# The first block's output projection in high and low parts instead of full-width fp32 products

## What is computed

```python
mod = silu(c) @ w_ada + b_ada            # six vectors of 1024: sh1, sc1, g1, sh2, sc2, g2
merged = concatenate([rmsnorm(lru_out), rmsnorm(attn_out)], axis=-1)    # 256 x 1024
y = merged @ w_out                        # 1024 x 1024, fp32
x = layernorm(DEEPNORM_ALPHA * x + g1 * y)
u = modulate(x, sh2, sc2)                 # input of the mixture of experts
```

## Time and profile before

| | before |
|---|---|
| device time, median of 3 runs | 3467.67 us |
| lowest and highest of them | 3466.52 and 3473.76 us |
| the profiled execution: first to last instruction | 3464.7 us |
| TensorE busy, VectorE busy, ScalarE busy | 91%, 67%, 46% |
| this stage, first DMA issue to the last residual instruction | 191.3 to 226.7 us |

### The profile page before, as it was taken

How to read it: one execution, slowest core, us unless ns; L and a number is a source line. 1 busy time by engine, 2 the same in 40 slices (tenths; PEclk the granted TensorE clock), 3 DMA queues, 4 the chain that set the end, 5 groups by cost and what they waited for, 6 DMA issues and landing times. The chain is left out here.

```text
span 3464.7 us, 62893 instructions
## 1 busy us (share of the span) xinstructions
PE 3157.3 (91%) x26416; PEld 2942.4 (85%) x26416; DVE 2335.4 (67%) x3486; ACT 1580.8 (46%) x2255; POOL 130.5 (4%) x148
## 2 busy tenths in 40 slices
PE   7679999889987799999989899999899999978899
PEld 5568777789876789999987899999699998867899
DVE  6547999767774467677577577775667677564544
ACT  3326777644551244544552444444644444432443
POOL 0000000000102000000000000000000001011000
PEclk9778999989997989999996899999899999989899
DMA  9336999757520047677430277675157575310242
GB/s 391 138 134 263 368 370 365 291 211 303 204 104 2 2 191 305 244 289 295 173 146 1 116 281 277 249 303 194 40 226 303 224 304 227 112 38 2 110 183 85
DMA packets 74502, 698.32 MB, mean 202 GB/s; under 512 B 8096, under 2 KB 12192, under 8 KB 50848
## 3 DMA queue, kind: packets, MB, share of 16 engines
q1 hardware_dynamic: 31360, 533.52, 39.3%
q10 hardware_dynamic: 41760, 153.11, 11.6%
q0 software_dynamic: 1152, 8.39, 0.6%
HBM read 690.79 MB, written 4.19 MB: 201 GB/s over the span
## 5 line engine op out<-in xcount | busy, mean ns | idle before, releaser
L1186 DVE TENSOR_TENSOR w_split<-ring,w_split 128x1024 fp32r<-128x1024 f32 x513 | 626.3, 1223 | 407.6 <-ACT w_split L1097 405.1
L1097 ACT ACTIVATE w_split<-ring 128x1024 fp32r<-128x1024 f32 x513 | 540.6, 1056 | 774.7 <-PE banks L1027 580.6
L1025 PE MATMUL banks<-u_split,w_split 128*128 128x256 f32 x2816 | 805.7, 286 | 14.7 <-DVE u_split L1246 12.9
L1026 PE MATMUL banks<-u_split,w_split 128*128 128x256 f32 x2816 | 803.8, 285 | 0.0
L1027 PE MATMUL banks<-u_split,w_split 128*128 128x256 f32 x2816 | 803.5, 285 | 0.0
L1025 PEld LDWEIGHTS banks<-u_split,w_split 128*128 128x128 f32 x2816 | 548.2, 195 | 19.4 <-DVE w_split L1186 10.0
L1026 PEld LDWEIGHTS banks<-u_split,w_split 128*128 128x128 f32 x2816 | 548.1, 195 | 0.4
L1027 PEld LDWEIGHTS banks<-u_split,w_split 128*128 128x128 f32 x2816 | 547.7, 195 | 0.0
L584 DVE CUSTOM_DVE_ANT_0 bufs<-bufs 128x1024 f32<-128x1024 f32 x332 | 395.0, 1226 | 41.9 <-DMA bufs<-ada 25.0
L1025 PE MATMUL banks<-h_split,w_split 128*128 128x256 f32 x1408 | 398.7, 283 | 1.8 <-DVE w_split L1186 1.8
L1026 PE MATMUL banks<-h_split,w_split 128*128 128x256 f32 x1408 | 398.4, 283 | 0.0
(11 more groups left out here) (472 smaller groups left out, 5067.5 us busy)
## 6 DMA issues: line engine op xcount, KB each, us to landing
ring<-stream SPq DMA_DIRECT2D x155, 3072.0 KB, 10.9
bufs<-ada ACTq DMA_DIRECT2D x288, 512.0 KB, 10.6
bufs<-ada SPq DMA_DIRECT2D x7, 2048.0 KB, 11.9
bufs<-ada POOLq DMA_DIRECT2D x8, 1024.0 KB, 8.3
ring<-stream SPq DMA_DIRECT2D x2, 2688.0 KB, 9.7
bufs<-c_rows SPq DMA_DIRECT2D x9, 512.0 KB, 4.5
ring<-stream SPq DMA_DIRECT2D x1, 2704.0 KB, 12.9
ring<-stream SPq DMA_DIRECT2D x1, 2176.0 KB, 7.8
```

The lines of the kernel that those rows point to most:

```text
L1025: pe.matmul(out, w(0), x(0), start=start, stop=False, skip_group_check=True)
L1026: pe.matmul(out, w(0), x(1), start=False, stop=False, skip_group_check=True)
L1097: nc.scalar.activation(w_split[:, slot, 0, :], piece(j, b), ACT.Copy).then_inc(high.sem, 1)
L1186: e = nc.vector.tensor_tensor(w_split[:, slot, 1, :], piece(j, b), w_split[:, slot, 0, :].bitcast(F32), ALU.subtract)
```

## The change

The projection is done in high and low parts. TensorE makes 192 products in fp32r (24 a block) in place of 64 in fp32. ScalarE, which had nothing in this stage, makes four high parts of the activations (128x512 each) and eight of the weights. VectorE makes four low parts of the activations, in place over `merged`, and eight of the weights: those of blocks 0 to 2 ahead of the modulation sums, those of blocks 3 to 7 between the quarters: behind the second and fourth quarter of slabs one and two and behind the second of slab three. SP's list is as it was. What `project_first_pair`, `project_split`, `weight_high` and `weight_low` do is described above.

```diff
@@ first_output_stage @@
+    high, low, w_slots = core.split_buf(1), core.split_buf(0), core.weight_slots(2)
+    keys = [("w_out", j) for j in range(KC)]
...
         @block.tensor
         def _(pe):
-            for j in range(KC):
-                core.project(pe, ("w_out", j), lambda k: merged[:, k, :], y[:, j, :], projected)
+            project_first_pair(core, pe, keys[0:2], w_slots, (high, low), core.psum[:, 0, :], u_low, projected, per=2)
+            for b in range(2, KC):
+                project_split(core, pe, b, keys[b], w_slots, (high, low), y[:, b, :], projected)
             after.on_tensor(pe)
+
+        @block.scalar
+        def _(act):
+            for c in range(0, KC, 2):
+                act.activation(high[:, c:c + 2, :], merged[:, c:c + 2, :], ACT.Copy).then_inc(u_high.sem, u_high.count(1))
+                if c in (0, 2):
+                    weight_high(core, act, c // 2, keys[c // 2], w_slots, projected)
+            for b in range(2, KC):
+                weight_high(core, act, b, keys[b], w_slots, projected)
 
         @block.vector
         def _(dve):
             link = chain(core, dve, "dve")
             pre(dve, link)
+            for c in range(0, KC, 2):
+                dve.wait_ge(u_high.sem, u_high.at(c // 2 + 1))
+                dve.tensor_tensor(low[:, c:c + 2, :], merged[:, c:c + 2, :], high[:, c:c + 2, :].bitcast(F32), ALU.subtract)\
+                    .then_inc(u_low.sem, u_low.count(1))
+                if c in (0, 2):
+                    weight_low(core, dve, c // 2, keys[c // 2], w_slots)
+            weight_low(core, dve, 2, keys[2], w_slots)
             for k in range(count):
                 dve.wait_ge(ada_loaded[k % 2].sem, ada_loaded[k % 2].at(16 * (k // 2 + 1)))
                 for q in range(4):
                     at = 4 * (first + k) + q
                     ada_quarter(core, dve, q, slots[k % 2], c_row, core.mod_sums[:, at:at + 1])
+                    if q in (1, 3) and 2 * k + q // 2 < KC - 3:
+                        weight_low(core, dve, 2 * k + q // 2 + 3, keys[2 * k + q // 2 + 3], w_slots)
```

More of the change, by code:

```diff
@@ L1664, in first_output_stage @@
     first, count = FIRST_HALVES + SECOND_HALVES, 12 - FIRST_HALVES - SECOND_HALVES
+    high, low, w_slots = core.split_buf(1), core.split_buf(0), core.weight_slots(2)
+    keys = [("w_out", j) for j in range(KC)]
     with core.nc.Block() as block:
         projected, step = core.event("projected"), core.event("ada_step")
+        u_high, u_low = core.event("u_high"), core.event("u_low")
         ada_loaded = [core.event(f"ada_loaded{q}") for q in range(2)]
```

## The result

| | before | changed |
|---|---|---|
| device time, median of 12 runs | 3463.51 us | 3474.61 us |
| ratio of changed to before | | 1.0038 (1.0024 to 1.0051) |
| the same, compared a second time | | 1.0026 (1.0015 to 1.0037) |
| profiled execution, first to last instruction | 3464.7 us | 3471.8 us |

The change makes the kernel slower by 0.26 to 0.38%, 9 to 13 us. The prediction was 3476.4 us in a range of 3470.0 to 3479.5, 8.75 us over before. One run of the changed kernel took 8920.83 us, over twice the others; it is left out of the ratios. (The brackets behind a ratio are its 95% interval.)

What follows compares the result with a forecast made beforehand. The prediction took VectorE's chain through SP's slab requests to bound the projection stage. A residual 5.6 us later plus token sums 3.15 us slower made 8.75 us on a median of 3467.67: 3476.4 us, range 3470 to 3479.5.

Steps and rivals of the forecast that it cites:

- What bounds the stage: Projection stage: VectorE's chain through SP's requests for slabs three and four ends it, within 1 us of TensorE's chain.
- TensorE's part: Projection products: first one 4.87 us after the stage's start, last near 223.2; even with VectorE free only 0.9 us to win.
- The head of VectorE's list at no cost: Before slab one: seven low parts, 5.8 us, fit inside VectorE's wait of 7.28 us and cost nothing.
- The wait for the fourth high part: After two quarters of slab one: VectorE idles 3.1 us for ScalarE, delaying SP's requests for slabs three and four.
- Slab four's landing: End of VectorE's chain: slab four lands 8.56 us after its request, at 224.25, so the residual starts 5.6 us later.
- The clock: Token sums behind the projection: TensorE's clock falls in a 6.4 us pause, so they take 6.90 us, adding 3.15 us.
- the chance of 0.2 for its holding: Rival for the token sums: the clock stays full through the pause, saving 3.15 us, result 3473.3 us; chance 0.2.
- Sum: Whole kernel: 5.6 us for the later residual plus 3.15 us for slower token sums, 8.75 us, giving 3476.4 us.
- Rival 2: VectorE's low part of block 3: no stall for its high part, 2.7 us cost, 3470.4 or 3473.5 us; chance 0.12.
- rival 3: Whole kernel faster: TensorE's own end moves by 0.9 us, to 3466.8 us at best; chance 0.03.
- rival 4: Projection blocks at half clock: more stalls, TensorE ends the stage at 229 to 234.8, 3476 to 3482 us; chance 0.07.

Runs made afterwards that it cites:

- three_slabs_fp32: The kernel before (fp32 products) with a third buffer for the slabs of modulation weights; ratio 0.9988, 65.32 us for the stage and the norms behind it.
- no_late_low_parts: The changed kernel without the low parts of weight blocks 3 to 7 and TensorE's products of them; ratio 1.0025, 69.98 us for stage and norms.
- changed_again: The changed kernel itself, unaltered, compared with the kernel before a second time; ratio 1.0026, 75.38 us for stage and norms.
- clock_fillers: The changed kernel with 40 products of zeros on TensorE between its last product and the token sums; ratio 1.0002, 72.85 us for stage and norms.
- more_high_slots: The changed kernel with five slots for the weights' high parts instead of three; ratio 1.0023, 72.39 us for stage and norms.
- norm_fillers: three_slabs_fp32 with products of zeros in TensorE's pauses in the centre stages behind the projection; ratio 0.9973, 65.35 us for stage and norms.
- split_three_slabs: The changed kernel with a third slab buffer, a fourth high-part slot and low parts 3 to 7 moved; ratio 0.9997, 70.30 us for stage and norms.

## Why the prediction was right

**What bounds the stage.** Right: VectorE's chain through SP's requests. three_slabs_fp32 shows it by removing the wait for a buffer.

**TensorE's part.** Right. First product 4.9 us after the stage's start (worked out 4.87), last one ended at 223.4 (223.2).

**The head of VectorE's list at no cost.** Right, and no_late_low_parts shows it alone. The margin was 0.45 us, not the 1.4 worked out, because slab one landed in 7.65 us instead of 8.56.

**The wait for the fourth high part.** Right in place, cause and size: the low part starts at 205.27 (205.28), after 3.62 us (3.1, slab one being earlier). SP's requests fell at 208.81 and 215.66 (208.8 and 215.7). The stage started 0.28 us later in this execution, so counted from its start each of these came 0.3 us sooner than worked out.

**Slab four's landing.** This term was too large. I took 8.56 us, the load with another behind it; it took 7.80, near the lower of the bounds. The Trainium skill says that on each DMA engine the descriptors of one row's ring are consumed in order (DMA: Bandwidth & Descriptors, "Queues, rings and completion order"), and the trace agrees: with the 3 MB unit requested 0.37 us behind it slab four took 7.80 us, as slab three took 7.77 with nothing behind it. It took 7.84, 7.83 and 7.93 us in changed_again, clock_fillers and no_late_low_parts, but 8.56 in more_high_slots, which none of my runs explains. I had let slab one's row speak against the rule. It isn't chance alone: slab one reached VectorE 7.64 to 7.80 us after its request in six executions of split kernels, slab two just as close behind, but after 8.56 us in the kernel before. With a third slab requested behind them it was 9.12 and 9.52 us with fp32 products (three_slabs_fp32, norm_fillers), and at most 8.26 in the two split kernels. So a row of the fp32 form was a poor price for the split form; why the two differ stays open. With the stage's later start of 0.28 us the term is 4.52 us for 5.6.

**The clock.** Right in size, 3.26 us for 3.15, and clock_fillers shows the cause. That it fell in the pause was in part luck. I had worked out a pause of 6.4 us, and it was 5.40, inside the 5.2 to 5.9 us where by my own figures either could happen. The 5.9 was misread, too: it is the length of TensorE's pause there, and the mean of 0.85 from 3226 to 3229 puts the fall at 3228.1, 5.3 us after the last work at 3222.75. So no pause of the trace had held the clock for 5.9 us, and the chance of 0.2 for its holding leaned on that. It fell 4.7 us after the last product here (223.4 to 228.1), and 3.5 and 2.7 us after it in more_high_slots and split_three_slabs. So a pause of 2.05 us cost 2.7 us in the sums (6.46 against 3.73), nearly as much as one of 5.4, and my thought that a shorter pause would save it failed twice.

**Sum.** 7.8 us in the trace for 8.75 predicted; 9 to 13 by the ratios, of which 1 to 5 us are unexplained. Both ratios are above 0.2%, though the interval of the second reaches down to 0.15%. That the absolute time came within 1.8 us (3474.61 for 3476.4) is partly luck: the base of 3467.67 was the median of 3 runs, 4.2 us above that of 12, and the rise of the medians was 11.1 us for 8.75. Rival 2 (no stall), rival 3 (faster) and rival 4 (TensorE the bound) didn't occur. The 0.9 us that rival 3 allowed at best are not passed by the best split form either, which is 0.6 us under before.

## What to carry to other kernels

Before work is put into the gaps of an engine's list, look at who is waiting for that engine: a gap that is a wait for a transfer can be filled freely ahead of that transfer's landing (the seven early low parts), but work that stands behind the landing and ahead of the instructions that free the buffer delays the request of the next transfer. Of two orders with the same instructions, the one that frees buffers first was 6.9 us shorter here. And if a change makes TensorE finish well before its next work can start, ask what clock that work will get; a few products into an unused bank can be cheaper than the pause (14 of them took 3.3 us off the measure), and too many hold up what stands behind.

## Not expected

The length of TensorE's pause says little about whether the clock holds: it was lost in the sums behind a pause of 2.05 us (split_three_slabs, 6.46 us of sums), and held in the kernel before behind one of 1.56 us (3.73 us), where it fell at 227.8, just as the sums ended. What else than the pause's length decides it, these runs don't show. The stretches behind the stage scatter by 3 and by 9 us between executions of kernels that are the same there, which is as large as the effect studied, so that device time alone would need many runs, where the measure in one trace agreed to 0.02 us between two executions of the changed kernel.
